# Mixture-of-experts passes taken in an order sorted on the chip, with three pass sizes and a new row order for the second matrix

## What is computed

```python
logits = hf @ router_w + router_b               # 256 tokens x 32 experts
top_val, top_idx = lax.top_k(logits, 4)
gate = softmax(top_val)
# for each expert e, over the tokens that chose it:
gu = xk @ w1[e] + b1[e]                         # 1024 -> 2048
g, u = min(gu[:, :1024], 7), clip(gu[:, 1024:], -7, 7)
y = ((u + 1) * g * sigmoid(1.702 * g)) @ w2[e] + b2[e]    # 1024 -> 1024
out[token] += gate * y
```

## Time and profile before

| | |
|---|---|
| median of the timed runs | 1293.68 us |
| the profiled execution's own time | 1293.53 us |
| its span, first to last instruction | 1291.8 us |
| PE matmuls busy | 1164.7 us, 90% of the span |
| DVE busy | 350.4 us, 27% |
| ACT busy | 178.2 us, 14% |
| read from HBM | 455.93 MB |
| weight chunks of experts | 396, which is 33 passes of 12 |
| granted TensorE clock, mean | 0.981 of full |

### The profile page before, as it was taken

The page is one execution under the profiler, slowest core; times in us unless marked ns, Lnnn a source line. Parts: engine busy times, 40 slices in busy tenths (PEclk is TensorE's granted clock), DMA queues, the critical chain, the costliest instruction groups (busy, mean ns, idle before and its releaser), DMA issues.

```text
span 1291.8 us, 18444 instructions
## 1 busy us (share of the span) xinstructions
PE 1164.7 (90%) x6596; PEld 506.2 (39%) x6597; DVE 350.4 (27%) x838; ACT 178.2 (14%) x365; POOL 6.9 (1%) x18
## 2 busy tenths in 40 slices
PE   4899987999999999999999888889889889999985
PEld 2577562443334344333333323333323334333332
DVE  3444454212323122122232222222222222122212
ACT  2233241010101010011010101111010100011001
POOL 1000000000000000000000000000000000000000
PEclk9999997999999999999999999999999999999998
DMA  9963963969999987699999999999999999999930
GB/s 351 295 244 102 386 278 154 348 231 378 418 417 419 418 339 252 248 417 418 418 418 418 417 417 417 417 418 419 418 418 418 418 418 418 358 415 418 418 143 32
DMA packets 101704, 457.34 MB, mean 354 GB/s; under 512 B 9496, under 2 KB 30096, under 8 KB 64784
## 3 DMA queue, kind: packets, MB, share of 16 engines
q1 hardware_dynamic: 100080, 456.29, 89.1%
q10 hardware_dynamic: 1600, 0.71, 0.2%
HBM read 455.93 MB, written 1.05 MB: 354 GB/s over the span
## 4 chain that ended last, share of the span: by engine, by line
PE 64%; DMA 15%; SPq 10%; DVE 5%; issue 4%; ACT 1%; ACTq 1%; DVEq 0%
PE bank L1144 29%; PE bank L1167 16%; DMA ring<-in_exp_w 13%; SPq L263 10%; PE bank L1014 5%; PE bank L1122 3%; PE bank L996 2%; PE bank L1035 2%; PE bank L962 2%; DVE scratch L837 2%; PE bank L1120 1%; DMA xg<-in_conf_dw_w 1%; PE bank L1154 1%; PE bank L1110 1%; PE bank L1134 1%
## 5 line engine op out<-in xcount | busy, mean ns | idle before, releaser
L1144 PE MATMUL bank<-ring,xg 128*64 128x512 f32 (+1 forms) x2112 | 544.6, 597 | 18.6 <-DMA ring<-in_exp_w 18.5
L1144 PEld LDWEIGHTS bank<-ring,xg 128*64 128x64 f32 (+1 forms) x2112 | 183.0, 145 | 358.3 <-issue 293.2
L1167 PE MATMUL bank<-ring,actT 128*64 128x512 f32 (+1 forms) x1056 | 273.7, 601 | 6.8 <-ACT actT L501 6.8
L1167 PEld LDWEIGHTS bank<-ring,actT 128*64 128x64 f32 (+1 forms) x1056 | 96.0, 147 | 163.6 <-issue 160.1
L494 ACT ACTIVATE act<-scratch 128x256 f32<-128x256 f32 (+1 forms) x66 | 29.7, 450 | 879.9 <-DVE scratch L837 879.9
L837 DVE TENSOR_SCALAR scratch<-bank 128x256 f32<-128x256 f32 (+1 forms) x66 | 30.4, 460 | 364.8 <-PE bank L1144 364.8
L827 DVE SCALAR_TENSOR_TENSOR acc<-bank,gate,acc 128x512 f32<-128x512 f32 x136 | 93.2, 744 | 106.2 <-PE bank L1122 89.7
L856 DVE TENSOR_TENSOR ysb<-bank,g2half 128x512 f32<-128x512 f32 x28 | 19.4, 692 | 226.4 <-PE bank L1167 226.4
L1110 PEld LDWEIGHTS bank<-onehot_bf,arena 128*128 128x128 bf16 x1584 | 55.6, 99 | 26.4 <-issue 26.4
L1154 PE MATMUL bank<-ident,act 128*128 128x128 f32 x152 | 28.7, 308 | 37.3 <-DVE act L847 32.4
L1014 PE MATMUL bank<-hT,ring 128*128 128x256 f32 x256 | 58.8, 390 | 3.7 <-DVE wcol L606 3.7
(11 more groups left out here) (191 smaller groups left out, 494.1 us busy)
## 6 DMA issues: line engine op xcount, KB each, us to landing
ring<-in_exp_w SPq DMA_DIRECT2D x396, 1024.0 KB, 17.8
ring<-in_ada_w SPq DMA_DIRECT2D x24, 1024.0 KB, 9.6
ring<-in_conf_pw_w SPq DMA_DIRECT2D x12, 1024.0 KB, 11.1
acc<-in_x SPq DMA_DIRECT2D x1, 1024.0 KB, 5.1
out<-acc SPq DMA_DIRECT2D x2, 512.0 KB, 2.7
g2full<-in_ada_b SPq DMA_DIRECT2D x1, 512.0 KB, 4.3
xT<-in_final_norm_g ACTq DMA_DIRECT2D x1, 512.0 KB, 3.9
b1f<-in_exp_b SPq DMA_DIRECT2D x1, 256.0 KB, 4.2
```

Source lines behind the costliest of these rows:

```text
L1144: ins = mm(dst, xg[:, b, k, 0:m], wk[:, n * F + h * H:n * F + (h + 1) * H], start=False, stop=(k == KT - 1))
L1167: ins = mm(dst, lhsT, wk[:, f % 2 * D + r * H:f % 2 * D + (r + 1) * H], start=(f == 0), stop=(f == KT - 1))
```

## The change

Three sizes of pass take the place of two: 32, 64 and 128 rows (`SMALL`, `MIDDLE`, `WIDE`). Which two are to be had depends on the position in the order: passes at odd positions (1, 3, 5, ...) are 64 or 128 rows, those at even positions 32 or 64. DVE sorts the experts by their counts (expert 0 stays first) and deals them out: the 15 with most rows to odd positions 3 to 31, the seven largest of them to 5, 9, ..., 29 and the next eight to 3, 7, ..., 31; the 16 with fewest to the even positions. SP loads experts by this order, after a wait for `s_seq`, read with one register load in each pass. PE, ACT and SP wait for the four increments of `s_seq` before their loops; DVE reads four more registers in each iteration.

In a pass of 32 rows `up` makes four matmuls of 256 columns for each half of a chunk, each with 32 stationary columns and in a column group of its own, and `down` puts its even and odd row blocks into different 32-row groups of the bank; the scatter adds the two. The activations are a quarter as long as in a wide pass.

The repeated pass has 64 rows, unless the expert has more than 192. Its preparation is a function (`prepare_extra`).

A chunk of `exp_w2` now takes rows in pairs: partition p holds rows 2p and 2p+1, one piece of 8 KiB. The transposes take every second activation column to match.

```diff
-            w2_rows = exp_w2[0].rearrange("e (q a p) n -> e q p a n", p=P, a=2)
+            w2_rows = exp_w2[0].rearrange("e (q p a) n -> e q p (a n)", p=P, a=2)
...
-            with sp.Fori(0, E) as e:
-                expert(e, e)
-
-            sp.wait_ge(s_tab, 1)
+            expert(0, 0)
+            sp.wait_ge(s_seq, 4)
+            with sp.Fori(1, E) as i:
+                e = sp.value_load(nexte[0:1, bass.ds(i, 1)], min_val=0, max_val=E - 1)
+                expert(i, e)
...
+        SIZES = [(MIDDLE, WIDE), (SMALL, MIDDLE)]
+        TOPS = E // 2 - 1
+        LATE = TOPS // 2
...
+        def parts(m):
+
+            return 2 if m == WIDE else P // m
+
+        def span(m):
+
+            return D // parts(m)
+
+        def up_to(m, n, r):
+
+            return bank[2 * r + n][:, :] if m == WIDE else bank[n][m * r:m * r + m, 0:span(m)]
...
-            step(v.tensor_scalar(wide[:, 1:E + 1], counts, float(NARROW), None, ALU.is_gt))
-            link(v.tensor_scalar(over[:, :], counts, float(WIDE), None, ALU.is_gt))
-            link(v.tensor_reduce(most[:, :], over[:, :], AX.X, ALU.add))
-            step(v.tensor_scalar(wide[:, E + 1:E + 2], most[:, :], 0.0, None, ALU.is_gt))
-            v.tensor_copy(extras[:, :], most[:, :]).then_inc(s_tab, 1)
+            v.tensor_scalar(wide[:, 1:2], counts[:, 0:1], float(MIDDLE), None, ALU.is_gt).then_inc(s_tab, 1)
+            step(v.scalar_tensor_tensor(out=key[:, :], in0=counts, scalar=float(E), in1=tie[:, :],
+                                        op0=ALU.mult, op1=ALU.add))
+            step(v.tensor_scalar(over[:, :], counts, float(WIDE), None, ALU.is_gt))
+            step(v.tensor_scalar(over2[:, :], counts, float(WIDE + MIDDLE), None, ALU.is_gt))
...
+            v.wait_ge(dve, n[0])
+            for r in range(E // 8):
+                at = slice(8 * r, 8 * r + 8)
+                link(v.max(ranked[:, at], key[:, :]))
+                link(v.max_index(ranked_e[:, at], ranked[:, at], key[:, :]))
+                if r < E // 8 - 1:
+                    link(v.match_replace(key[:, :], ranked[:, at], key[:, :], -float(E * E * E * E)))
+            late, early, rest_e = slice(0, LATE), slice(LATE, TOPS), slice(TOPS, E - 1)
+            for where, ranks, most_rows in ((slice(3, E + 1, 4), early, MIDDLE), (slice(5, E + 1, 4), late, MIDDLE),
+                                            (slice(2, E + 1, 2), rest_e, SMALL)):
+                step(v.tensor_scalar(wide[:, where], ranked[:, ranks], E * (most_rows + 1) - 0.5, None, ALU.is_gt))
+                step(v.tensor_scalar(seq[:, where], ranked_e[:, ranks], 1.0, None, ALU.add))
+                step(v.tensor_copy(nexte[0:1, slice(where.start - 1, E, where.step)], ranked_e[0:1, ranks]))
+            link(v.tensor_reduce(most[:, :], over2[:, :], AX.X, ALU.add))
+            v.tensor_scalar(wide[:, E + 1:E + 2], most[:, :], 0.0, None, ALU.is_gt).then_inc(s_seq, 1)
+            link(v.tensor_reduce(extra_n[:, :], over[:, :], AX.X, ALU.add))
+            v.tensor_copy(extras[:, :], extra_n[:, :]).then_inc(s_seq, 1)
...
+            link(v.scalar_tensor_tensor(out=first[:, :], in0=over2[:, :], scalar=2.0 * E, in1=first[:, :],
+                                        op0=ALU.mult, op1=ALU.add))
...
+            link(v.tensor_scalar(orderw[:, :], order[:, :], 2.0 * E, None, ALU.is_gt))
+            v.tensor_copy(xwide[:, :], orderw[0:1, :]).then_inc(s_seq, 1)
+            link(v.scalar_tensor_tensor(out=order[:, :], in0=orderw[:, :], scalar=-2.0 * E, in1=order[:, :],
+                                        op0=ALU.mult, op1=ALU.add))
+            v.tensor_scalar(eidx[:, :], order[0:1, :], -1.0, float(E), ALU.mult, ALU.add).then_inc(s_seq, 1)
+            v.wait_ge(s_seq, 4)
...
+                es = [v.value_load(seq[0:1, bass.ds(it * UNROLL + j, 1)], min_val=0, max_val=E + 1)
+                      for j in range(UNROLL + 2)]
...
                     for n in range(2):
-                        for h in range(2):
-                            m, dst = (WIDE, bank[2 * h + n][:, :]) if w else (NARROW, bank[n][64 * h:64 * h + 64, :])
-                            ins = mm(dst, xg[:, b, k, 0:m], wk[:, n * F + h * H:n * F + (h + 1) * H],
+                        for r in range(parts(m)):
+                            at = n * F + r * span(m)
+                            ins = mm(up_to(m, n, r), xg[:, b, k, 0:m], wk[:, at:at + span(m)],
                                      start=False, stop=(k == KT - 1))
                     ins.then_inc(used, 1)
...
-                q = 4 if w else 2
+                q = KT * m // WIDE // 2
...
+                    at = f // (2 * q) * m
+                    sides = 2 if m == SMALL else 1
+                    row = m * (f % sides)
                     for r in range(2):
...
+                        dst = bank[2 + r][:, :] if m == WIDE else bank[2][64 * r + row:64 * r + row + m, :]
+                        ins = mm(dst, actT[:, f % (2 * q), at:at + m], wk[:, f % 2 * D + r * H:f % 2 * D + (r + 1) * H],
+                                 start=(f < sides), stop=(f >= KT - sides))
...
+            pe.wait_ge(s_seq, 4)
             with pe.Fori(0, E // UNROLL) as it:
```

More of the change, by code:

```diff
@@ L514, in _ @@
             oT_out(1, 0)
-            either(a, w0, lambda w: xg_out(1, 0, w))
+            either(a, w0, SIZES[0], lambda m: xg_out(1, 0, m))
+            a.wait_ge(s_seq, 4)
             with a.Fori(0, E // UNROLL) as it:
@@ L557, in _ @@
             step(v.memset(wide[:, :], 0))
+            step(v.memset(seq[:, 0:1], 0))
+            step(v.memset(seq[:, 1:2], 1))
+            step(v.memset(seq[:, E + 1:E + 2], E + 1))
             v.memset(eps[:, :], EPS).then_inc(s_const_v, 1)
@@ L889, in _ @@
-            step(v.tensor_copy(bsel[:, E:E + 1], bsel[:, bass.ds(e0, 1)]))
+            prepare_extra(e0)
+            v.wait_ge(s_xcol, 1)
             take_b2()
@@ L1101, in turn_onehot, with gather @@
                 ins.then_inc(oT_done, 1)
-            def gather(b, w):
-                m = WIDE if w else NARROW
+            def gather(b, m):
                 per = 512 // m
@@ L1141, in up, with down @@
                     for n in range(2):
-                        for h in range(2):
-                            m, dst = (WIDE, bank[2 * h + n][:, :]) if w else (NARROW, bank[n][64 * h:64 * h + 64, :])
-                            ins = mm(dst, xg[:, b, k, 0:m], wk[:, n * F + h * H:n * F + (h + 1) * H],
+                        for r in range(parts(m)):
+                            at = n * F + r * span(m)
+                            ins = mm(up_to(m, n, r), xg[:, b, k, 0:m], wk[:, at:at + span(m)],
                                      start=False, stop=(k == KT - 1))
                     ins.then_inc(used, 1)
-            def down(i, i2, w):
-                q = 4 if w else 2
+            def down(i, i2, m):
+                q = KT * m // WIDE // 2
                 for h in range(2):
@@ L1153, in down @@
                     for n in range(q):
-                        ins = tr(bank[5 - h][:, n * P:(n + 1) * P], act[:, (h * q + n) * P:(h * q + n + 1) * P],
+                        ins = tr(bank[5 - h][:, n * P:(n + 1) * P], act[:, bass.ds((h * q + n - n % 2) * P + n % 2, P, 2) if q > 1 else slice(h * P, h * P + P)],
                                  ident[:, :])
@@ L1207, in _ @@
             pe.wait_ge(s_lov, 2)
[L1208 removed]
+            either(pe, w0, SIZES[0], lambda m: gather(0, m))
             pe.wait_ge(s_gate, TT)
@@ L1242, in _, with all_up @@
                         turn_onehot(0)
-                        gather(0, True)
+                        either(pe, xw, SIZES[0], lambda m: gather(0, m))
                     pe.wait_ge(xg_ready, i + (E + 1))
                     pe.wait_ge(y_ready, i + (E + 1))
-                    up_bias(0, True)
-                    up(i + E, 0, True, range(KT))
+                    def all_up(m):
+                        up_bias(0, m)
+                        up(i + E, 0, m, range(KT))
+                    either(pe, xw, SIZES[0], all_up)
                     pe.wait_ge(acc_done, i * 2 + (2 * E + 3))
-                    down(i + E, i * 2 + 2 * E, True)
+                    either(pe, xw, SIZES[0], lambda m: down(i + E, i * 2 + 2 * E, m))
                     pe.wait_ge(y_ready, i + (E + 2))
                     pe.wait_ge(oT_ready, i + (E + 1))
-                    scatter(0, True)
+                    either(pe, xw, SIZES[0], lambda m: scatter(0, m))
 _INS = ["x", "c", "ada_w", "ada_b", "mix_norm_g", "ffn_norm_g", "conf_pw1_w", "conf_pw1_b", "conf_dw_w",
```

199 lines of the change are left out of this document (110 added, 89 removed).

## The result

The changed kernel takes 1223.22 us (four runs, 1221.67 to 1224.63) against 1294.2 us of the kernel before in the same comparison; the ratio is 0.9454, 95% interval 0.9443 to 0.9465. The profiled execution has a span of 1221.5 us. That is 71 us less than before, where 95 were forecast, and outside the range of 1189 to 1221.

The account below looks back on a forecast made before the run. The prediction took the expert part to be bound by chunk transfers. Its terms, 213.7 + 5.6 + 955.3 + 5 + 2.5 + 15.0, gave a span of 1197.1 us, with 1.7 around it 1198.8 us; range 1189 to 1221.

Parts of the forecast that it names:

- The stream was the bound: Expert part: chunk transfers, not PE, set the pace; 402.7 MB at 421.5 GB/s take 955.3 us.
- Small passes: 32-row passes at all 16 even positions: 16.4 us of PE work each, where a 64-row pass takes 26.8 us.
- Row pairs: Second matrix's chunks in 8 KiB pieces: stream time 955.3 us in place of 963.3; rival that they do not help, chance 0.10.
- The order: Wide passes each between small ones: a group of four costs PE 115 us against 119.4 us of transfers, so the stream hardly stops.
- The sorting: DVE's ranking ahead of the loop: 6.8 us of steps, PE's first bias matmul and the stream 5.6 us later; ends 3 and 12.
- One sum beside the forecast: Alternative estimate for 4 KiB pieces: 1.1% dearer than 8 KiB ones, so the time would come out 6 us later than forecast.
- Stops at wide passes and in the first pass: Stream standing still: 1 us for each of four wide passes and 1 for the first pass, 5 us; ends 0 and 20.
- The clock: Rival: small passes run at 1.2 GHz, taking 29.3 us each, and the time is about 1255; chance 0.05.
- more branches: Listed under costs at nothing, with extra register loads; without PE's spare time as cover, a microsecond per iteration would add 16.
- The end: After the last landing: 2.5 us for the last two row blocks and semaphore, then 15.0 us to the end.
- of which everything but the last chunk hides under its own transfers: Repeated pass, now 64 rows: of its 26.8 us of work only the last chunk's comes after the stream's end.
- The other rivals: Overlap only of two, 1245, chance 0.04; no row-pair help, 1207, 0.10; repeated pass still wide or other sizes, 1221, 0.02.

Follow-up runs that it names:

- swapped: The changed kernel with sizes of odd and even positions exchanged, wide passes at positions 4, 8, 12 and 16: 1196.28 us, ratio 0.9239.
- warm_end: The changed kernel with eight extra bfloat16 matmuls, their result unread, behind the last matmul of every pass at an even position: 1215.93 us, ratio 0.9404.
- fixed_tail: The changed kernel with PE's repeated pass written out for 64 rows without branches: 1217.13 us, ratio 0.9408.

## Why the prediction was wrong

The mechanism was right, and most terms. The stream was the bound, at 421.5 GB/s (measured 422). Small passes cost what the column groups in the convolution said: 16.4 us and 1.7 for the wide scatter make 18.1, and behind a wide pass `swapped` took 17.9 to 18.0. Row pairs gave the expected rate. The order did remove most of the standing still: some 61 us before, about 24 now. The sorting cost 5.2 to 5.9 us where 5.6 were forecast, with the ranking 1.1 us too long in the sum and the cold first chunks not in it. That the restart came only 3.55 us later is the luck of this execution, which had reached the top-4 search 2.3 us earlier. One sum beside the forecast is off: 1.1% of the third of the stream that is `exp_w2` saves 3.5 us, which is 4.5 us later than the forecast and not 6.

Two terms were mis-sized, and together they are more than the whole miss.

*Stops at wide passes and in the first pass: 5 us forecast, about 24 measured.* The step that failed is the one that took 1 us for each wide pass, between the ends 0 and 4.5. The lone wide pass of the kernel before lost 4.5 us, as a row, and I argued it down with the small pass behind it. That half was right: behind a wide pass the loss fell from 3.4 us (368 GB/s from 1110.9 to 1139.5 us in the kernel before) to between 1.0 and 1.8. But I gave a wide pass its old 51.6 us and its old start. In fact it began 2.4 to 2.6 us behind the last matmul, at half clock, and took 53.3 to 55.7 us. Both come of the idle time at the loop's head. That head was at nothing, under "more branches", and it was longer than before by some 1 us. The clock stood among the rivals at 0.05, priced for small passes that run slow; ahead of the wide passes they hardly did, and where they do (0.90 from 900 to 1000 us) it is hidden. The sentence that a wide pass is dense and brings the clock back was true (0.56 in its first 6.7 us, 1.00 in the next 7) and missed that the time until it is back lies in the one pass without slack. The measured shares of the 21.7 us: `swapped` takes away 18.8 with clock and start together. `warm_end` takes away some 10 with the clock, which leaves some 8 to the start. That division is rough, since loops of this order lost between 18.4 and 21.7 us in three profiles, and two of the four wide passes of `warm_end` still ran at 0.94.

*The end: 17.5 us forecast from the last landing, 25.1 measured.* The failed step is "of which everything but the last chunk hides under its own transfers". It took for granted that PE reaches the repeated pass before its chunks do. The branches that the change puts into this pass left PE idle for 5.9 us just there, and PE was done 9.1 us behind the stream where 2.5 were forecast. By `fixed_tail` 3.4 us of that go with the gap. The other 3.2 stay without it: `down` waits for the activations, starts late and does not hide under its transfers. The last 1.0 us lies behind PE's end, where the shorter scatter and `ysb` step saved 1.3 us and not 2.3. In the costs at nothing, "more branches" stood with the cover that PE has time to spare inside the loop; the repeated pass lies outside it.

The sum closes: restart 2 us earlier than forecast, stops 19 us more, end 7.6 us more, 24.4 us in all, which is 1221.5 - 1197.1. The range failed for the same reason: each of its upper bounds was there (stops up to 20, the end wide), but it did not let two of them come together.

The other rivals are settled: matmuls in four column groups do overlap (0.90 us a chunk, as in the earlier trace rows), the row pairs do help, and the repeated pass did become one of 64 rows.

## What to carry to other kernels

When a stream of transfers sets the pace and one kind of pass runs longer than its share, the lead in slots is a budget: add up not only the pass's own excess but its late start, the register loads and branches ahead of it, and a clock that idle time ahead of it has let fall. Put the long pass in the middle of a loop's body, behind work without a gap. And count code as a resource: a branch that copies a body can turn a loop that was loaded once into one that is loaded in every iteration, and a body outside the loop is cheapest straight. Before reading a difference of 2 or 3 us out of two profiles, look for a point that the change can't have moved and count from there.

## What was not expected of the hardware

A PE loop whose body grew by two branched copies went from 19 to 148 packets of code and from 1223 to 1383 us. The head of PE's loop left it idle for 1.0 us when it was behind the stream and for up to 2.8 us when it had just waited for a chunk, and over a gap of 2.6 us the granted clock fell from 1.00 to half. Eight matmuls that compute nothing, in such a gap ahead of a dense stretch, made a kernel 7 us faster. And pieces of 8 KiB moved at 420 to 422 GB/s where two pieces of 4 KiB per partition moved at 409.
